# Last feed-forward up projection by seven quarter products in place of eight, with its own weight and bank plan

## The reference

```python
def swiglu(h, w_up, w_down):
    g, u = jnp.split(h @ w_up, 2, axis=-1)
    return (jax.nn.silu(g) * u) @ w_down
...
x = x + mix
x = x + swiglu(rmsnorm(x, norm_ffn[layer]), ffn_w_up[layer], ffn_w_down[layer])
```

## Time and profile before

| | us |
|---|---|
| median of three runs (2453.25 to 2456.48) | 2454.54 |
| the profiled execution, its own time | 2453.33 |
| its span | 2451.5 |
| PE busy | 2423.9 (99%) |
| VectorE, ScalarE, GpSimd busy | 969.0, 868.1, 1159.7 |

### The profile page before, as it was taken

How to read it: one execution, slowest core, us unless ns; L and a number is a source line. 1 busy time by engine, 2 the same in 40 slices (tenths; PEclk the granted TensorE clock), 3 DMA queues, 4 the chain that set the end, 5 groups by cost and what they waited for, 6 DMA issues and landing times.

```text
span 2451.5 us, 37584 instructions
## 1 busy us (share of the span) xinstructions
PE 2423.9 (99%) x15528; PEld 2187.7 (89%) x15528; DVE 969.0 (40%) x1712; ACT 868.1 (35%) x1153; POOL 1159.7 (47%) x933
## 2 busy tenths in 40 slices
PE   9999999999999999999999999999999999999998
PEld 6899987787887988999999989988888889999998
DVE  4513246344435344433343434344433534222324
ACT  5431235243223365433333243354422324222223
POOL 3722147655555444635445550064455544544453
PEclk9999999999999999999999999999999999999999
DMA  9863373322323588322223274422242344223222
GB/s 330 303 225 139 141 250 121 125 69 78 116 79 134 172 279 265 123 79 86 87 72 102 97 273 168 161 91 81 74 132 96 104 155 138 87 95 95 87 87 87
DMA packets 102249, 335.91 MB, mean 137 GB/s; under 512 B 12288, under 2 KB 16192, under 8 KB 102080
## 3 DMA queue, kind: packets, MB, share of 16 engines
q1 hardware_dynamic: 102080, 333.52, 40.2%
HBM read 255.20 MB, written 76.16 MB: 135 GB/s over the span
## 4 chain that ended last, share of the span: by engine, by line
PE 91%; DVE 4%; POOL 2%; issue 1%; ACT 1%; DVEq 1%; DMA 1%; POOLq 0%; SPq 0%; ACTq 0%
PE ps L825 65%; PE ps L891 19%; POOL wl L1461 1%; PE ps L931 1%; PE ps L987 1%; PE ps L985 1%; DVE mixl L1845 0%; POOLq L1467 0%; PE ps L907 0%; PE ps L1048 0%; PE ps L1045 0%; PE ps L991 0%; PE ps L942 0%; POOL rsA L1473 0%; DMA wr<-in_wblk 0%
## 5 line engine op out<-in xcount | busy, mean ns | idle before, releaser
L1461 POOL TENSOR_TENSOR wl<-wr,wh 128x512 fp32r<-128x512 f32 x656 | 858.5, 1338 | 501.9 <-ACT wh L1191 501.4
L825 PE MATMUL ps<-xh,wh 128*128 128x260 f32 (+2 forms) x3296 | 881.2, 322 | 7.6 <-DVE xA L1855 2.2
L825 PE MATMUL ps<-xl,wh 128*128 128x260 f32 (+2 forms) x3296 | 867.7, 318 | 0.0
L825 PE MATMUL ps<-xh,wl 128*128 128x260 f32 (+1 forms) x3280 | 866.0, 319 | 0.0
L825 PEld LDWEIGHTS ps<-xh,wh 128*128 128x128 f32 (+1 forms) x3296 | 543.0, 187 | 62.1 <-issue 18.9
L825 PEld LDWEIGHTS ps<-xl,wh 128*128 128x128 f32 (+1 forms) x3296 | 542.5, 187 | 44.7 <-issue 2.4
L825 PEld LDWEIGHTS ps<-xh,wl 128*128 128x128 f32 x3280 | 540.8, 188 | 44.5
L1191 ACT ACTIVATE wh<-wr 128x1024 fp32r<-128x1024 f32 (+1 forms) x332 | 342.7, 1044 | 281.0 <-DMA wr<-in_wblk 276.8
L891 PE MATMUL ps<-hidh,wh 128*128 128x260 f32 (+1 forms) x1024 | 277.2, 324 | 6.8 <-POOL wl L1461 3.0
L891 PE MATMUL ps<-hidl,wh 128*128 128x260 f32 (+1 forms) x1024 | 274.0, 321 | 0.0
L891 PE MATMUL ps<-hidh,wl 128*128 128x260 f32 (+1 forms) x1024 | 273.4, 320 | 0.0
(11 more groups left out here) (375 smaller groups left out, 2269.2 us busy)
## 6 DMA issues: line engine op xcount, KB each, us to landing
wr<-in_wblk SPq DMA_DIRECT2D x328, 512.0 KB, 3.8
split<-wh SPq DMA_DIRECT2D x64, 512.0 KB, 5.5
split<-wl SPq DMA_DIRECT2D x64, 512.0 KB, 6.7
wh<-split SPq DMA_DIRECT2D x64, 512.0 KB, 3.3
wl<-split SPq DMA_DIRECT2D x64, 512.0 KB, 4.2
xr<-in_xT SPq DMA_DIRECT2D x8, 260.0 KB, 5.8
xB<-in_xT SPq DMA_DIRECT2D x8, 260.0 KB, 5.8
out_yT<-xB SPq DMA_DIRECT2D x8, 260.0 KB, 2.3
```

What stands on the lines that cost most here:

```text
L825: mm = pe.matmul(ps[0:cols, b + c, 0:n], wt[:, w], xt[:, e:e + n], start=first, stop=end)
L1461: last = pool.tensor_tensor(lo[:, e], raw[:, e], hi[:, e].bitcast(F32), ALU.subtract)
```

## The change

**Seven products.** In the last FFN (layer 1, B) the gate and up units of one hidden block f (22 of them) are one product of a 2x2 matrix of weight quarters (gate or up, lower or upper half of k) and a 2x2 matrix of x quarters (half of k, half of the columns). It is made by seven products of quarters in the form of Strassen and Winograd. Each is a unit `sp` of one bank: four tiles of k, three matmuls of 260 columns each. Four sums of weight quarters (`wS`, DVE, 512 columns each) are made per f, and four sums of x quarters once (`xt`). Set f is loaded as two blocks (`wq`), after the third product of set f-2; all seven quarters and sums that are used get high parts (`wH`, ACT: 1024, 512, 1024 and 1024 columns) and low parts (`wP`, POOL, seven pieces of 512; for odd f DVE makes the last two as one piece of 1024, `wL`). ACT copies the first two products to SBUF, DVE adds the other five; then Silu, one product over 520 columns on DVE (`s_hm`), and hidh and hidl as before.

**Norm factor.** x of B is multiplied by the norm's gain and its factor before it is split (`xn`, DVE; `xh` ACT and `xl` DVE in seven quarters of 1040 columns), so the evacuation multiplies by no factor, and POOL's product of the gate is gone there.

**Banks.** The last FFN uses six banks as three pairs: products take turns in two pairs, down units in all three.

**Order.** The eight `out` units of layer 1, B stand ahead of the down units 8 of FFN A; the split of x and of the first two weight sets stands beside the end of FFN A. The squares and the final scaling of A stand in the last FFN. Down weights of the last FFN have slots and splits of their own (`wd`, `wD`).

**Elsewhere.** A weight block that follows two neighbouring `up` units is split ahead of the second one's evacuation instead of behind it; POOL makes every low part of 1024 columns in one instruction instead of two.

```diff
+PIECE = (0, 3, 1, 4, 5, 6, 7)
+PSTEP = (0, 1, 0, 2, 2, 3, 3)
+XPIECE = (0, 2, 1, 3, 4, 5, 6)
+PAIRS = ((0, 2), (3, 4), (4, 6), (6, 8))
...
+    def last_ffn(at):
+        for f in range(NF):
+            g, kk = f // 2, f % 2
+            for i in range(7):
+                add(("sp", f, i))
+                if i == 1 and f and (kk or f == 2):
+                    add(("hl", 1, B, (f - 1) // 2, (f - 1) % 2))
+                if i == 2 and f + 2 < NF:
+                    add(("wq", f + 2))
+                for s in at.get((f, i), ()):
+                    add(s)
+            add(("hh", 1, B, g, kk))
...
+            if kk and g:
+                for m in range(KT):
+                    add(("down", 1, B, g - 1, m))
+                    if m == 1:
+                        add(("hl", 1, B, g, 1))
...
+            put(f - 1, (0,), ("wS", f, 0))
+            put(f - 1, (2,), ("wS", f, 1), ("wP", f, 0), ("wP", f, 1), ("wH", f, 2))
+            put(f - 1, (3,), ("wP", f, 2), ("wH", f, 3))
+            put(f, (0,), ("wL", f, 3))
+        else:
+            put(f - 1, (0,), ("wS", f, 0))
+            put(f - 1, (1,), ("wH", f, 0))
+            put(f - 1, (2,), ("wH", f, 1))
+            put(f - 1, (3,), ("wS", f, 1))
+            put(f - 1, (5,), ("wH", f, 2), ("wP", f, 0), ("wP", f, 1))
+            put(f - 1, (6,), ("wH", f, 3), ("wP", f, 2))
+            put(f - 1, ("down", 2), ("wP", f, 3))
+    for g in range(NG):
+        first, second = ((2 * g + 2, 5), (2 * g + 3, 0)) if g < NG - 1 else ((NF - 1, 3), (NF - 1, 5))
+        put(first[0], first[1:], ("wD", g, 0))
+        put(second[0], second[1:], ("wD", g, 1))
...
+def banks_of(g):
+    return (0, 1, 2) if g % 2 == 0 else (1, 0, 2)
+def product_bank(f, i):
+    x, y, z = banks_of(f // 2)
+    one, two = (y, z) if f % 2 else (x, y)
+    return (2 * one + 1, 2 * one, 2 * one + 1, 2 * two + 1, 2 * two, 2 * one, 2 * one + 1)[i]
...
-            b = cur % 4
-            cur += nb
+            elif k == "down" and x[1:3] == (1, B):
+                b = 2 * banks_of(x[3] + 1)[(0, 2, 1)[x[4] % 3]]
...
-                after.setdefault(u + (4 if short else 1), []).append(("w", n))
+                if name[u][0] == "up" and name[u + 1][0] == "up":
+                    ahead.setdefault(u + 1, []).append(("w", n))
+                else:
+                    after.setdefault(u + (4 if short else 1), []).append(("w", n))
...
+            def product(u, f, i):
+                pe.wait_ge(s_qhi, 4 * f + PSTEP[i] + 1)
...
+                for k in range(KT // 2):
+                    w, e = slice(PIECE[i] * 512 + k * P, PIECE[i] * 512 + (k + 1) * P), slice(k * Q, (k + 1) * Q)
+                    xh, xl = xqh[XPIECE[i]], xql[XPIECE[i]]
+                    for wt, xt, first, end in ((wqh[f % 2], xh, k == 0, False), (wqh[f % 2], xl, False, False),
+                                               (wql[f % 2], xh, False, k == KT // 2 - 1)):
+                        mm = pe.matmul(ps[:, b, 0:Q], wt[:, w], xt[:, e], start=first, stop=end)
...
-                for e in (slice(0, w // 2), slice(w // 2, w)):
-                    last = pool.tensor_tensor(lo[:, e], raw[:, e], hi[:, e].bitcast(F32), ALU.subtract)
-                last.then_inc(s_lo, 1)
+                pool.tensor_tensor(lo, raw, hi.bitcast(F32), ALU.subtract).then_inc(s_lo, 1)
...
+            def set_sums(f, part):
+                v.drain()
+                if part == 0:
+                    v.wait_ge(s_wq[f % 2], 32 * (f // 2 + 1))
+                    v.tensor_tensor(s1, a21, a22, ALU.add)
+                    v.tensor_tensor(s3, a11, a21, ALU.subtract)
+                else:
+                    v.tensor_tensor(s2, s1, a11, ALU.subtract)
+                    v.drain()
+                    v.tensor_tensor(s4, a12, s2, ALU.subtract).then_inc(s_wsum, 1)
...
+            def products_sum(it, f, i):
...
+                elif i == 4:
+                    v.tensor_tensor(t5[:], part, u1, ALU.add).then_inc(s_evd, 1)
+                    v.tensor_tensor(r, r, u1, ALU.add)
+                elif i == 5:
+                    v.tensor_tensor(gsum[:, Q:2 * Q], part, t5[:], ALU.add).then_inc(s_evd, 1)
+                else:
+                    v.tensor_tensor(hf[:, t:t + Q], part, r, ALU.add)
+                    v.tensor_tensor(hf[:, t + Q:t + 2 * Q], part, t5[:], ALU.add).then_inc(s_evd, 1)
+                    v.drain()
+                    v.wait_ge(s_gsi, f + 1)
+                    v.tensor_tensor(hf[:, t:t + 2 * Q], hf[:, t:t + 2 * Q], gsum[:], ALU.mult).then_inc(s_hm, 1)
```

More of the change, by code:

```diff
@@ L84, in ffn @@
                     add(("nrm", N_FFN[L, X]))
+            for s in at.get((g, "end"), ()):
+                add(s)
             if g:
@@ L87, in ffn @@
                     add(("down", L, X, g - 1, m))
+                    for s in at.get((g, "down", m), ()):
+                        add(s)
                     if m == 1:
@@ L117, in ffn @@
         for m in range(KT):
             add(("down", L, X, NG - 1, m))
-            if m % 2:
+            for s in at.get((NG, "down", m), ()):
+                add(s)
+            if m % 2 and n_next:
                 add(("xs", n_next, m // 2))
+    def last_ffn(at):
[8 more added lines that the diff above has]
+                for s in at.get((f, i), ()):
+                    add(s)
+            add(("hh", 1, B, g, kk))
+            if f + 2 == NF:
+                add(("wd", NG - 1))
+            if kk and g:
[3 more added lines that the diff above has]
+                        add(("hl", 1, B, g, 1))
+                    for s in at.get((f, "down", m), ()):
+                        add(s)
+                if g + 1 < NG:
+                    add(("wd", g))
+        for c in range(2):
+            for m in range(KT):
+                add(("dh", c, B, m))
+                if m:
+                    add(("xe", c, m - 1))
+                if c and m == 2:
+                    add(("ne", 0))
+                if c and m == 4:
+                    add(("nr",))
+                if c and m == 6:
+                    add(("nl",))
+                    add(("nx", 4))
+            add(("xe", c, KT - 1))
+        add(("nx", 5))
+        add(("nx", 6))
+        add(("nx", 7))
+        add(("fe", 0))
+        add(("ne", 1))
+        add(("fe", 1))
@@ new lines, in order @@
+    for g in range(NG):
+        first, second = ((2 * g + 2, 5), (2 * g + 3, 0)) if g < NG - 1 else ((NF - 1, 3), (NF - 1, 5))
+        put(first[0], first[1:], ("wD", g, 0))
+        put(second[0], second[1:], ("wD", g, 1))
+    for m in range(KT):
+        put(2 * m + 3, ("down", 5), ("xs", 8, m))
+    put(18, (0,), ("nrm", 8), ("nrv", 8))
+    for m in range(KT):
+        put(19 + 2 * (m // 4), ("down", 2 * (m % 4)), ("fin", m))
+        if m % 2:
+            put(19 + 2 * (m // 4), ("down", 2 * (m % 4)), ("fo", m - 1))
@@ L289, in __init__ @@
                 self.rs_end[x[1]] = rs_cur[NORMS[x[1]][0]]
-            if k not in ("sm", "in", "z", "out", "up", "down", "dh", "rg", "s1"):
+            if k not in ("sm", "in", "z", "out", "up", "down", "dh", "rg", "s1", "sp"):
                 continue
@@ L327, in __init__ @@
                 new = [NB * x[1] + B_FFN + (0 if g == 0 else 4 + (g - 1) * 6) + q]
[L328 to L336, removed]
+            elif k in ("sp", "dh") or k == "down" and x[1:3] == (1, B):
+                continue
             elif k == "down":
@@ L354, in __init__ @@
         self.n_units = n_units
-        after, name = {}, {u: x for x, u in self.u.items()}
+        after, name, ahead = {}, {u: x for x, u in self.u.items()}, {}
         for n in range(len(self.blocks)):
@@ L885, in down @@
                 for k in range(2):
[L886 removed]
+                    hi, lo_ = down_weights(u, L, X, g, k)
+                    w = slice(m * P, (m + 1) * P)
                     t = (2 * (g % 2) + k) * W[X]
[L888 to L889 removed]
+                    for wt, xt, first, end in ((hi, hidh, k == 0, False), (hi, hidl, False, False),
+                                               (lo_, hidh, False, k == 1)):
                         for c, lo, n in pieces(X):
@@ L1026, in gla_sample_end @@
                     pe.wait_ge(s_q2, 1)
-                    pe.matmul(ps[:, 5, 64:128], ones, osq[:], start=True, stop=True).then_inc(s_qm2, 1)
+                    pe.matmul(ps[:, 5, 64:128], ones, osq[:], start=True, stop=True).then_inc(s_qm, 1)
             def mlstm_columns(X):
```

325 lines of the change are left out of this document (261 added, 64 removed), and 9 rows, old and new, of the table outs.

## The result

The changed kernel takes 2469.47 us (median of 4, 2468.50 to 2471.29), beside 2455.51 us for the kernel before on the same chip: ratio 1.0062, 95% interval 1.0050 to 1.0074. It is 0.6% slower, where 2443 us, 0.5% faster, had been forecast. The profiled execution took 2471.29 us, its span is 2469.5 us against 2451.5 before: 18.0 us more.

What follows compares the result with a forecast made beforehand. The prediction took PE's matmuls as the bound (busy 99% of the span); -31.7 + 20 - 2 + 2 + 1.5 - 1 = -11.2 us gave 2443 us, 0.5% faster, with an 8-in-10 range of 2423 to 2465 us.

Steps and rivals of the forecast that it cites:

- Matmuls: Last FFN: seven products replace two up units, 84 matmuls for 96, in 22 blocks: -31.7 us.
- The mechanism and the queue: Odd blocks: DVE's two-operand SBUF instructions wait for POOL, DVE's queue makes PE late 2.0 us per group: +20 us.
- a lone one 0.3 us: Odd block's queue: a DVE instruction not following straight on another waits 0.3 us for POOL, instead of 1.05.
- Product 2's wait: Groups: PE waits for ACT's copy of product 0; more than 0.3 us would show the queue wrong.
- The start: Beside A's last 16 down units: DVE has 22 us of work before waits; +2 us, between 0 and 8.
- The instruction of 1024 columns gives the same work: POOL's whole-block low parts: DVE's lone waits may double, mostly under longer units; 0, at worst +4 us.
- the wait for xl: First up unit of the last FFN: PE's 2.0 us wait, caused by DVE scaling A's output, goes: -2 us.
- Norm of A: Block 18: norm work in ACT's queue delays DVE's sums and POOL's pieces for block 19: +1.5 us once, 0 to 4.
- Gate blocks split ahead: Elsewhere: earlier splitting saves only PE's waits for low parts: -1 us, 0 to -3.
- Loads, ACT, POOL by throughput: Per group of 31.8 us: loads covered, ACT 14 us, POOL 20.8 us; all hide by throughput.
- VectorE becomes the bound: Rival, chance 0.20: POOL still runs at odd blocks' second sums, down unit 0 4.1 us late; 2465 us.
- The sets' loads: Rival, chance 0.05: weight sets taking over 12 us to land hold DVE's queue at its first sum; about 2455 us.

Runs made afterwards that it cites:

- e3: Changed kernel with POOL filling the last FFN's weight low parts with zeros by memset instead of subtracting, true low parts left out: 2428.53 us, 0.9893.
- e4: Changed kernel with hidh of even blocks placed behind ACT's copy of the next block's first product: 2468.52 us, 1.0054.
- e1: Changed kernel with POOL's low parts of 1024-column blocks made as two instructions of 512 again: 2464.95 us, 1.0043.
- e6: Changed kernel with norm-factor products and first sums of x quarters moved ahead of group 10's first gate evacuation: 2465.84 us, 1.0044.
- e9: Changed kernel with e1's edit, Silu's output in PSUM for the gate product, and more of x's work ahead of A's last down units: 2447.30 us, 0.9968.
- e2: Changed kernel with gate blocks split behind the second up unit's evacuation again: 2472.83 us, 1.0076.
- e11: Changed kernel with POOL's low parts in the last FFN cut into pieces of 256 columns, twice as many: 2468.83 us, 1.0054.
- e10: e9 without ACT's copy of product 1; DVE adds that product from its bank behind product 3: 2469.22 us, 1.0066.

## Why the prediction was wrong, point by point

- **Matmuls**, -31.7: right. e3's groups of 31.74 us have exactly the demand that was computed (31.8), and the 84 of an even block took 10.07 us.
- **The mechanism and the queue**: right, the size too small. Ends in the odd block, forecast and measured from 2208.24: gate product 2.15 and 2.36; low part of 1024 columns 4.4 and 4.6; first two sums 7.9 and 8.0; hidl 9.65 and 9.7; add of product 2 10.1 and 10.3; then product 4 12.4 and 12.9, product 6 14.5 and 15.45, gate product 15.5 and 17.05, down unit 0 16.2 and 17.6. The term that failed is "a lone one 0.3 us". The lone gate product and the last sum of 260 columns were held 0.72 and 0.5 us in the mean (1417 and 923 ns against 700 and 420), and 0.8 to 0.9 each in this block:

```profile
2221.04 1.29 DVE L2000 TENSOR_TENSOR p<-p,p 128x260 f32<-128x260 f32 x1
...
2223.78 1.51 DVE L2008 TENSOR_TENSOR hf<-hf,gsum 128x520 f32<-128x520 f32 x1
```

  The forecast took the 0.3 from hidl's 709 ns before. But of those 21 instructions 20 ran with POOL idle, at 0.69 us; the only one that met POOL's instruction, 0.51 us before its end, took 1.07:

```profile
2079.01 2.53 POOL L1461 TENSOR_TENSOR wl<-wr,wh 128x512 fp32r<-128x512 f32 x2
...
2081.03 1.07 DVE L1874 TENSOR_TENSOR hidl<-hf,hidh 128x520 fp32r<-128x520 f32 x1 [0.71 <-ACT hidh L1320]
```

  So that mean told how seldom the two met, not what a meeting costs. In the new order 15 of the 16 gate products looked at meet a POOL instruction with 0.85 to 0.95 us left. Down unit 0 is then done at 17.6, which down unit 3 wants at 14.4: 3.2 us late instead of 1.8. PE's waits in the four places, 3.15 us, are the parts of this one lateness; that it does not add up over the places was right, as e4 bears out. Over nine groups and their small gaps it is 32 us instead of 18.
- **Product 2's wait**, at most 0.3: 0.69, because the gate product ahead of ACT's work was held (1.47 us in the block shown). e4 shows that removing it moves it to product 6.
- **The start**, +2 (0 to 8): **+13.1**, in proportion the largest error. The forecast's queue began with the down units, as 22 us on DVE beside 22 of PE, and lateness there was given to four banks. But DVE came to them late: 9.1 of the 13.3 us of hold stand before 2038 us, on instructions that the order places in the up units of group 10, where DVE scales x and makes its sums. These holds were in no term, and the upper bound of 8 us was seven holds of 1.05, all in the down units. "The instruction of 1024 columns gives the same work" (0, at worst +4) made single holds 2.0 instead of 1.05 us, but undoing it (e1) is worth only 1.5 us of the start; moving the work ahead is worth 4.8 (e6) and some 5 (e9). The rest was not tried. The -2 for the wait for xl came as forecast: it is in the -2.9.
In the first, starts of 512-column matmuls lie 0.43 us apart instead of 0.23, for 20 of them; as DVE had no pause there, these 4 us do not show to be on the path. In the second, 26 matmuls of 260 columns lie 0.22 apart instead of 0.12: the first 168 start within 22.7 us instead of e3's 20.1, 2.6 us that are in the +4.9.
- **Norm of A**, +1.5: about 0.9. Its group took 37.48 us instead of 35.26; in e3, where DVE is not held, 33.03 instead of 31.76. **Gate blocks split ahead**, -1: e2 gives -3.4, just past the far end of 0 to -3; against the kernel before it was 1.2 us ahead at 1859 us, until the clock took that back. **Loads, ACT, POOL by throughput**: right, ACT 13.1 us of the forecast 14; POOL 25.5 instead of 20.8, its pieces lengthened to 1457 and 1840 ns by DVE.
- **The rivals.** The time is nearest to "VectorE becomes the bound" (2465), but its condition did not occur: POOL had run out before the second pair of sums (first of them 0.69 us at 2219.14). The sets' loads were never late.

By these sizes the sum would be -31.7 + 32 + 7.6 (first and last blocks) - 2.9 + 13.1 = +18.1, against 18.0 measured.

## What to carry to other kernels

When a change takes matmuls from a stage that PE bounds and pays in adds on DVE, write DVE's and POOL's queues out side by side, and let every two-operand SBUF instruction of DVE, lone ones too, wait for the end of the POOL instruction that runs when it starts. A mean from the old order does not give this: look at the single instructions that met POOL. Keep one operand in PSUM where a bank is free (11.8 us here for two instructions a group), and don't expect much of the width of POOL's instructions alone: in e11 narrow ones made POOL late, in e1 the kernel was 4.5 us faster, with 1.5 of them at the start. A stage's first operands are a term of their own: begin the count where DVE starts to fall behind, not where the stage before ends, and look at the granted clock behind long waits of PE (2.6 us here in the first two blocks).

## What was not expected of the hardware

A hold is about as long as the rest of the POOL instruction that runs when the DVE instruction starts: 0.1, 0.5, 0.7 and 1.2 us left gave 0.0, 0.4, 0.55 and 1.1 us of hold. Where POOL only wrote SBUF there was none at all (692 and 700 ns in e3). Smaller pieces cut the hold but cost POOL time: with no two-operand DVE instruction beside it a piece of 256 columns took 0.74 us (103 pieces of e11), one of 512 took 1.29 (14 pieces of the kernel after). And a wait of PE in a dense row of matmuls can cost clock, by no fixed amount: waits of 3.2 to 3.8 us at the start of the last FFN went with 3.4 (e2), 6.8 (e3) and 10.2 us (the kernel after) at half clock, and six of e10's ten waits of 2.9 us with 3.4 us.
